# Last-token matrices turned in block 0, the last two MoE blocks summed on 128 partitions, the last expert staged, and the final scaling shared with GpSimd

## The reference

```python
yb = lax.map(expert_block, ...)       # (silu(x @ w_gate[e]) * (x @ w_up[e])) @ w_down[e]
y_slot = yb[dest] * wts.reshape(-1)[order][:, None]
ffn = jax.ops.segment_sum(y_slot, tok, num_segments=n_tok)
x = x + gate2 * ffn.reshape(bsz, L, D_MODEL)
# final: y = x * rsqrt(mean(x * x) + eps) * norm_f_w
```

## Time and profile before

| | |
|---|---|
| median of 3 runs | 1455.46 us (1450.97 to 1467.53) |
| profiled execution | 1452.0 us |
| its span, first to last instruction | 1449.7 us |
| mean granted TensorE clock | 0.969 of full |
| PE matmul busy | 1358.5 us, 94% |
| DVE, ACT, POOL busy | 433.9, 265.5, 234.1 us |
| chain that ended last | PE 79%, DMA 8%, DVE 5%, issue 3% |
| DMA in total | 318.07 MB, mean 219 GB/s |

### The profile page before, as it was taken

How to read it: one execution, slowest core, us unless ns; L and a number is a source line. 1 busy time by engine, 2 the same in 40 slices (tenths; PEclk the granted TensorE clock), 3 DMA queues, 4 the chain that set the end, 5 groups by cost and what they waited for, 6 DMA issues and landing times.

```text
span 1449.7 us, 26021 instructions
## 1 busy us (share of the span) xinstructions
PE 1358.5 (94%) x10242; PEld 850.3 (59%) x10243; DVE 433.9 (30%) x913; ACT 265.5 (18%) x401; POOL 234.1 (16%) x280
## 2 busy tenths in 40 slices
PE   5898999978999999999969999999999999999975
PEld 3688778756787666664434455555555455554532
DVE  4792860375622412104462000000000000000065
ACT  3305012244125000000111111111111111111102
POOL 0043402200000000000005013003122222222320
PEclk9899899998999999999989999999999999999997
DMA  7459622345430212413168818917949999999993
GB/s 302 152 136 386 140 69 66 81 147 181 170 111 10 87 44 73 172 46 145 44 249 330 342 29 340 395 29 292 396 155 396 389 398 380 403 380 403 377 402 132
DMA packets 91756, 318.07 MB, mean 219 GB/s; under 512 B 11920, under 2 KB 12304, under 8 KB 91440
## 3 DMA queue, kind: packets, MB, share of 16 engines
q1 hardware_dynamic: 72304, 268.77, 48.9%
q0 software_dynamic: 10608, 34.19, 8.0%
q10 hardware_dynamic: 8784, 14.24, 3.2%
HBM read 281.99 MB, written 33.06 MB: 217 GB/s over the span
## 4 chain that ended last, share of the span: by engine, by line
PE 79%; DMA 8%; DVE 5%; issue 3%; ACT 2%; SPq 2%; POOL 0%; POOLq 0%; DVEq 0%; ACTq 0%
PE ps L2222 22%; PE ps L1762 11%; PE ps L2233 11%; PE ps L1750 10%; DMA expert_w<-in_w_down 5%; PE ps L2132 5%; PE ps L2183 4%; PE ps L1854 2%; PE ps L1937 2%; DMA expert_w<-in_w_up 2%; SPq L553 1%; PE ps L2228 1%; PE ps L2212 1%; PE ps L1777 1%; DMA x_sorted<-h,router_ints 1%
## 5 line engine op out<-in xcount | busy, mean ns | idle before, releaser
L2222 PE MATMUL ps<-expert_w,x_block_t 128*64 128x256 f32 x3584 | 405.8, 383 | 10.6 <-issue 6.7
L2222 PEld LDWEIGHTS ps<-expert_w,x_block_t 128*64 128x64 f32 x3584 | 257.2, 138 | 159.1 <-issue 33.7
L2233 PE MATMUL ps<-expert_w,act_t 128*64 128x512 f32 x896 | 212.7, 602 | 4.1 <-DMA expert_w<-in_w_down 3.7
L1762 PE MATMUL ps<-h_t,weight_ring 128*128 128x320 f32 x640 | 179.0, 436 | 0.1
L1762 PEld LDWEIGHTS ps<-h_t,weight_ring 128*128 128x128 f32 x640 | 121.6, 191 | 54.2 <-issue 7.6
L1750 PE MATMUL ps<-h_t,weight_ring 128*128 128x320 f32 x512 | 148.8, 454 | 2.8 <-ACT h_t L730 2.8
L1661 DVE TENSOR_TENSOR activations<-silu_tmp,ps 128x256 f32<-128x256 f32 x56 | 23.6, 422 | 375.7 <-ACT silu_tmp L948 375.6
L1750 PEld LDWEIGHTS ps<-h_t,weight_ring 128*128 128x128 f32 x512 | 102.0, 201 | 46.7 <-issue 9.3
L2233 PEld LDWEIGHTS ps<-expert_w,act_t 128*64 128x64 f32 x896 | 58.3, 137 | 101.4 <-issue 81.4
L673 POOL COPY expert_w<-staged 128x1024 f32<-128x1024 f32 x42 | 43.8, 1043 | 416.8 <-PE ps L2222 315.9
L1682 DVE COPY y_block<-ps 128x512 f32<-128x512 f32 x25 | 17.3, 692 | 187.5 <-PE ps L2233 187.5
(11 more groups left out here) (355 smaller groups left out, 1309.1 us busy)
## 6 DMA issues: line engine op xcount, KB each, us to landing
expert_w<-in_w_down SPq DMA_DIRECT2D x128, 512.0 KB, 13.6
weight_ring<-in_stream SPq DMA_DIRECT2D x98, 512.0 KB, 5.0
expert_w<-in_w_gate SPq DMA_DIRECT2D x58, 512.0 KB, 11.3
expert_w<-in_w_up SPq DMA_DIRECT2D x58, 512.0 KB, 12.3
staged<-in_w_gate SPq DMA_DIRECT2D x28, 512.0 KB, 13.9
gathered<-in_w_gate SPq DMA_DIRECT2D x28, 512.0 KB, 15.9
gathered<-in_w_up SPq DMA_DIRECT2D x28, 512.0 KB, 16.5
x_sorted<-zero POOLq DMA_DIRECT2D x18, 512.0 KB, 15.0
```

What stands on the lines that cost most here:

```text
L1762: last = mm(pair(job)[:, a, :], w[:, k, :], h_t[:, k, a * HALF:(a + 1) * HALF], start=(k == 0), stop=(k == KD - 1))
L2222: last = mm(ps[MB * g:MB * g + MB, 2 * half + w, 0:256], x_blk_t[:, 2 * kp + k2, :], rows[:, at_col:at_col + 256], start=(kp == 0 and k2 = ...
L2233: last = mm(ps[MB * half:MB * half + MB, 4, :], act_t[:, 4 * (f // 4) + 2 * (f % 2) + f // 2 % 2, :], w_slot[3 * f + 2][:, 4 * half:4 * ha ...
```

## The change

- The last expert is loaded like all others (`next_expert(n)` for n up to 15), with POOL's copies for it too. POOL's gathers therefore wait for `slot_filled >= EXPERTS * STAGED`, the last of these copies.
- The matrices of the last tokens are turned in block 0, behind the down slice 5, into banks 0 to 2, and DVE copies them. `pick_t` moves to memory that is free from then on.
- Block 26's result is copied to `y_blk` like the others'. SP then copies its two halves with two DMAs to the other half of the partitions (`y_swap`), and DVE multiplies them by the gate into the other half of `y_last` (`take_swapped`). So block 26 and block 27 stand on different partitions for the same columns, and one matmul with 128 partitions adds both: five chunks with two matmuls each, in banks 0, 2, 6, 4, 0.
- The 20 gather steps are spread as `((0, 0, 6), (2, 4, 8))`.
- In the final norm the reciprocals of two chunks come together; chunks 0, 2 and 4 are scaled by DVE, chunks 1 and 3 by POOL in two operations.

```diff
@@ SP
-                if staged == 0:
-                    for f in range(STAGED // 2):
-                        sp.wait_ge(gu_in[f], 64)
-                        sp.sem_inc(slot_filled, 2)
...
-            with sp.Fori(2, EXPERTS - 1) as n:
-                next_expert(n, STAGED)
-            with sp.Fori(EXPERTS - 1, EXPERTS) as n:
-                next_expert(n, 0)
+            with sp.Fori(2, EXPERTS) as n:
+                next_expert(n)
+            sp.wait_ge(y_raw_ready, 1)
+            for half in range(2):
+                sp.dma_start(y_swap[MB * (1 - half):MB * (2 - half), :], y_blk[MB * half:MB * half + MB, :])\
+                    .then_inc(y_swapped, 16)
             for c in range(CH):
-                sp.wait_ge(fin_ready, c + 1)
+                sp.wait_ge((fin_ready, fin_pool)[c % 2], c // 2 + 1)
@@ POOL
-            with pool.Fori(1, EXPERTS - 1) as n:
+            with pool.Fori(1, EXPERTS) as n:
...
-            pool.wait_ge(slot_filled, (EXPERTS - 1) * STAGED)
+            pool.wait_ge(slot_filled, EXPERTS * STAGED)
...
+            for c in (1, 3):
+                pool.wait_ge(std_inverse, c + 1)
+                nc.gpsimd.tensor_scalar(fin[c][:, :], fin[c][:, :], rms2[:, 24 + c:25 + c], None, ALU.mult)\
+                    .then_inc(pool_scaled, 1)
+                pool.wait_ge(pool_scaled, c // 2 + 1)
+                nc.gpsimd.tensor_tensor(fin[c][:, :], fin[c][:, :], nf_row[:, :], ALU.mult).then_inc(fin_pool, 1)
@@ ACT
-            act.wait_ge(pick_turned, 1)
-            turned = pick_t[:, :, :, :].rearrange("p u c t -> p (u c t)")
-            nc.scalar.activation(turned[:, 0:512], ps[:, 7, :], ACT.Copy)
...
@@ DVE
-                note(vec.tensor_tensor(pick[:, u, :, 0, :], hit1, hit2, ALU.add))
-                note(vec.tensor_tensor(pick[:, u, :, 1, :], hit1, hit2, ALU.add))
+                for half in range(2):
+                    note(vec.tensor_tensor(pick[:, half, :, u if half else 1 - u, :], hit1, hit2, ALU.add))
...
+            def take_swapped():
+                for half in range(2):
+                    rows = slice(MB * (1 - half), MB * (2 - half))
+                    note(vec.tensor_tensor(y_last[rows, half, :, :], bc(y_swap[rows, :], 1, 2),
+                                           g2_row[rows, :, 512 * half:512 * half + 512], ALU.mult))
...
+            dve.wait_ge(pick_turned, 1)
+            turned = pick_t[:, :, :, :].rearrange("p u c t -> p (u c t)")
+            vec.tensor_copy(turned[:, 0:1024].rearrange("p (a n) -> p a n", a=2), ps[:, 0:2, :])
+            vec.tensor_copy(turned[:, 1024:1280], ps[:, 2, 0:256]).then_inc(pick_taken, 1)
...
-            for u, (ahead, beside, behind) in enumerate(((0, 0, 6), (3, 6, 5))):
+            for u, (ahead, beside, behind) in enumerate(((0, 0, 6), (2, 4, 8))):
                 add_some(ahead)
                 dve.wait_ge(silu_ready, last2 * 2 + (2 * u + 1))
                 take_prod(0)
+                if u == 1:
+                    dve.wait_ge(y_swapped, 32)
+                    dve.wait_ge(slot_filled, EXPERTS * STAGED)
+                    take_swapped()
                 add_some(beside)
                 dve.wait_ge(silu_ready, last2 * 2 + (2 * u + 2))
                 take_prod(1)
                 add_some(behind)
                 dve.wait_ge(down_done, last2 * KF + (u * KF + KF))
-                take_last(u, 0)
-                take_last(u, 1)
-                dve.wait_ge(y_last_ready, 2 * u + 2)
-                vec.nop().then_inc(y_copied, 1)
...
+                if u == 0:
+                    dve.wait_ge(y_stored, last2 * 32 + 32)
+                    vec.tensor_copy(y_blk[:, :], ps[:, 4, :]).then_inc(y_copied, 1)
+                    dve.wait_ge(y_copied, last2 + 2)
+                    vec.nop().then_inc(y_raw_ready, 1)
+            settle()
+            take_last(0)
+            take_last(1)
...
+            add_last_rows(0)
+            add_last_rows(1)
+            invert(0)
+            invert(1)
+            scale_rows(0)
+            add_last_rows(2)
+            add_last_rows(3)
...
@@ PE
+                if f == KF - 3:
+                    pe.wait_ge(pick_ready, 1)
+                    for n in range(2 * CH):
+                        last = nc.tensor.transpose(ps[:, n // 4, (n % 4) * P:(n % 4 + 1) * P],
+                                                   pick[:, n // CH, n % CH, :, :].rearrange("p a t -> p (a t)"), ident)
+                    last.then_inc(pick_turned, 1)
...
+            for c in range(CH):
                 cv = 0 if c < SCH else 1
-                pe.wait_ge(y_last_ready, 2 * u + cv + 1)
+                pe.wait_ge(y_last_ready, (1, 1, 1, 2, 2)[c])
+                if c == CH - 1:
+                    pe.wait_ge(x3_ready, 1)
                 for half in range(2):
...
+                    last = mm(ps[:, (0, 2, 6, 4, 0)[c] + half, :], pick_t[:, half, c, :], y_last[:, half, cv, :],
+                              start=True, stop=True)
```

79 lines of the change are left out of this document (35 added, 44 removed).

## The result

The changed kernel takes 1470.69 us (median of 18 runs, 1463.25 to 1481.38) against 1453.91 us for the kernel before on the same chip (18 runs, 1449.04 to 1467.53): a ratio of 1.0117, 95% interval 1.0094 to 1.0139. It is 1.2% slower. I had said 1458, with a chance of 0.83 that the change stays within 1% of no difference; the range ended at 1470. The profiled execution took 1467.5 us with a span of 1465.7, 16.0 more than before.

A forecast was written before the change was run, and what follows sets the result against it. DMA was taken to bound the kernel up to the last product, a serial chain after it. 0 + 9.6 - 7.9 + 2.4 = +4.1 on 1452.0 gave 1456.1, or 1459.6 on the median; forecast 1458, range 1447 to 1470.

The forecast's parts named there:

- the swapped rows: Block 26's result swapped for DVE late in block 27: landing between 1411.3 and 1417.4, taken as 1412.0.
- the first sum: Ahead of the first final add: four matmul records of 0.45 us, 1.8 us, and 0.2 to hand over.
- Gathers and evacuation: Last two blocks: late gathers hold DVE, so the last block's evacuation starts at 1431.5, not 1421.9: +9.6 us.
- From evacuation to the first add: After the last product: half the evacuation and the transposes leave the path, 11.3 us becomes 3.4: -7.9.
- Final scaling: First final add to last scaling, shared by DVE and POOL: 13.46 us becomes 15.9, +2.4 (1.6 to 4).
- The tail: After the last scaling: no term in the sum; the last store's 3.05 us was noted in the kernel before.
- block 0's transposes: Ten transposes added in block 0, 1.3 us of PE time, absorbed by later waits for weights: taken as 0.
- the loop end: PE's 3.1 us of empty block-loop iterations lie beside the wait for DVE; in the open, the saving is 6.1.
- (a): Rival: gathers land quicker, 6.5 us in place of 10.1; 1449 profiled, 1452 on the median; chance 0.17.
- (b): Rival: DVE isn't held at all and the changed end stands alone, -17.6 us, 1438 on the median; chance 0.04.
- (d): Rival: transfers unchanged, DVE's delay and the saved end cancel, 1455 to 1456; chance 0.10.
- (c): Rival: same wait but longer, evacuation after 1442, +11.1 on top; 1467 profiled, 1471 median; chance 0.14.

The follow-up runs named there:

- e4: The kernel before with the last expert staged and nothing else, so the gathers go late; ratio 1.0047 to the kernel before.
- e7: The changed kernel with the last expert loaded directly as before and the two swap DMAs on ACT's queue; ratio 1.0053 to the kernel before.
- e3: The changed kernel with the last expert loaded directly as before, so the gathers go early; ratio 1.0119 to the kernel before.
- e10: The changed kernel with the last expert loaded directly, the swap DMAs on ACT's queue and the final scaling on DVE alone; ratio 0.9980 to the kernel before.
- e1: The changed kernel with the final norm back on DVE alone; ratio 1.0068 to the kernel before.
- e8: The changed kernel with all 20 gather steps put behind the last block's second product; ratio 1.0191 to the kernel before.
- e12: The changed kernel with the gather steps last, as in e8, and the swap DMAs on ACT's queue; ratio 1.0089 to the kernel before.
- e2: The kernel before with the shared final scaling on POOL and DVE added and nothing else; ratio 1.0046 to the kernel before.
- e9: The changed kernel with POOL scaling chunk 1 only and DVE taking chunk 3; ratio 1.0081 to the kernel before.

## Why the prediction was wrong

The hold ahead of the evacuation was foreseen; what failed is the pricing of the end behind it. The sum gave POOL's share of the final norm +2.4 us, and nothing for POOL's drain at the program's end. These two steps measured +5.9 (1.1 of it by the TensorE clock) and +4.05, and make up 7.6 us of the miss. The rest lies in two other terms: the swapped rows came later than I said, and the first sum took twice its time, 2.4 and 2.0 us.

On the profiled time the sum said +4.1 and +15.5 were measured (1452.0 to 1467.5). The gap of 11.4 lies in four terms.

**Gathers and evacuation, +9.6 said, +12.0 measured.** The mechanism was right nearly to the instruction: last copy 1388.7 said and 1387.4 measured, first gather 1389.1 and 1388.2, first scaling 1399.2 and 1398.66, first half product 1410.3 and 1409.73, PE standing over 10 us ahead of its turn. The 2.4 us come from the swapped rows: I put them at 1412.0, between 1411.3 and 1417.4, and they were there at 1414.20 (6.63 us from the second issue). That pushed chunk 2's end and so chunk 4's gather, from 1419.5 to 1421.9. These times flatter the forecast a little: everything from block 26 on was 1.4 us earlier in this execution than in the one that I reckoned from, and on that count the evacuation was 13.4 us late, not 12.0. The mechanism stands on it as well. That the time is this hold and not something else that happened with it is shown by e4 (the hold alone costs 9.3 us in the profile, 0.5% in time) and by e7 (without it and the swap's place on the queue the evacuation is back at 60.5). What I missed is that the swap on SP's queue becomes a hold of the same size once the last expert is loaded directly and the gathers are early: e3.

**From evacuation to the first add, -7.9 said, -5.9 measured.** The evacuation's half took 1.54 (1.4 said). The sum took from 1435.41 to 1439.27, 3.86, where I said 2.0. I had divided 5.43 us by twelve records and given each of the four new records that pace. But the old records have 64 rows and run in pairs side by side; a new one has 128. The groups of all forty records before and all twenty now (busy us, mean ns) show half the records in the same time.
```profile
L2311 PE MATMUL ps<-y_last,last_tokens_t 64*128 64x512 f32 x40 | 11.9, 743 | 2.4 <-ACT last_tokens_t L990 1.5 <-DVE final L1707 0.9
```
```profile
L2347 PE MATMUL ps<-y_last,last_tokens_t 128*128 128x512 f32 x20 | 11.8, 755 | 6.6 <-DVE y_last L1658 6.6
```
The comparison holds only at one clock, and both sums began at the lower level. In these windows the clock stands behind the five busy times, first the kernel before, then the changed one:
```profile
1427.00:1433.00 6.00, 5.26 (x14) 2.22 (x16) 0.00 (x0) 2.18 (x4) 0.00 (x0) 0.51 0.00 0
```
```profile
1435.00:1440.00 5.00, 4.59 (x6) 2.02 (x7) 2.37 (x4) 0.00 (x0) 0.00 (x0) 0.50 0.00 0
```
At that level a pair of 64-row records starts every 0.85 us before, and a single 128-row record every 0.85 now; where the clock is back at 1.00, both do every 0.43. So four new records need 3.9 us to the first add at the lower level, and at the upper one they would need about the 2.0 that I said, by luck, as my pace was that of the pairs at the lower. In the changed kernel the PE had stood 6.65 us ahead of the sum. In e10, where it had stood 3.31, the sum began at 1.00, fell to 0.50 after 1437, and the first add came 2.54 us after its start. The join on 128 partitions saves PE no time; in exchange it needs the swap.

**Final scaling, +2.4 said (1.6 to 4), +5.9 measured.** The range was wrong too. I took the multiply by the per-row scalar at one copy's time, 1.04, without a word on it, and bounded only the second operation, at 3.1. The second took 2.35, near my 2.1; the first took 3.80. POOL is done with chunk 3 at 18.3 after the first add, where I had 14.6, and DVE's last scaling, which starts at 16.0, takes 3.33 beside it. "GPSIMD Engine Reference" of the Trainium skill, Elementwise, by which I had estimated 2.25 for the two-input multiply, is near the measured 2.35. For the 3.80 I had no row.

The 3.80 isn't shown to be the operation's time alone. In all thirteen instances, in seven kernels, one of DVE's scalings was under way when it began, and ended 1.07 to 1.10 us later; the scalings that had begun ahead of POOL took no longer than alone (1.27 against 1.28 in e1). If POOL stood still for that time, as DVE does behind POOL's multiply by `norm_f`, the operation would take 2.7 alone; that is an estimate, and no run has it without a scaling of DVE. I had priced the turns on DVE's side only.

Not all of the +5.9 is POOL's. 1.1 us of it come from the sum of chunk 1, which at the lower clock was 2.78 us behind that of chunk 0, where I had 1.8. In e3, e8 and e12, with the same join and the same work on POOL but this sum only 1.64 to 1.83 us behind, the stretch takes 18.2 to 18.4; in e2, without the join, 17.9. e2 shows most of the term, 4.5 us, without the rest of the change.

**The tail, 0 said, +4.05 measured.** It wasn't in my sum. I gave the last store its 3.05 us and didn't ask what else the end of the program waits for. POOL, which used to go into its drain 46 us before the end, now works until 1457.5, a microsecond before DVE is done with the last chunk. e1, e2 and e9 show it from three sides.

Together 2.4 + 2.0 + 3.5 + 4.05 = 11.95, less 0.5 that lies outside the span (1.8 us now, 2.3 before).

**Right:** block 0's transposes cost nothing that can be seen. Block 2's gates start 58.2 us after the first scatter before and 57.7 after. From the scatter to block 26 it is 603.2 and 603.3, but this figure scatters by 3.3 us between the kernels, more than the 1.3 of the transposes; the DMA rate didn't change; the loop end is hidden by the late evacuation.

**The rivals.** (a) and (b) didn't happen: the first landing was 10.4 us after the first issue. (d) was true of the transfers but not of the rest. (c) named 1467 on the profiled time, and 1467.5 came, but not by its mechanism: it wanted the evacuation after 1442 (its own terms, added up, reach only 1441.0), and it came at 1433.9. The other terms, for which I had allowed 1.6 us in it, made the difference. Its chance, 0.14, was too low because I put all doubt into the waits and hardly any into the operations that no row showed.

**Open.** From the first add on POOL's share costs 9.9 us in the profile by e1, 8.5 by e2 and 8.7 by e10 against e7, the first with the 1.1 us of the clock in it. The timed ratios give 7 us for e1 and e2 and 10 for e10 against e7, and their intervals, some 5 us on either side with two ratios and 3.5 with one, don't tell these apart. What POOL's multiply by the per-row scalar takes alone isn't shown. Nor is it shown why the clock in the first sum differs between executions of one kernel.

## What to carry to other kernels

When a buffer is lent to a second user, ask what its first user is now late for, and then what is late next: here the late gathers held the end by some 10 us, and going back to direct loads alone gave nothing, as the swap then waited behind the weights for as long. An engine that is given work near the end brings its operations, the slowdown of the engines beside it, and its own wind-down at the program's last line; price all three. A small transfer on which the chain hangs belongs on a queue without bulk loads. And an operation that the trace doesn't show needs bounds that are really wide, one for each operation.

## What I had not expected of the hardware

- POOL's multiply of 128x1024 float32 by one value per partition took 3.80 us, each time with one of DVE's scalings under way for its first 1.1 us; its multiply of two such tiles took 2.35, its copy 1.04.
- POOL's drain at the program's end took 10.3 us and ended 7.9 to 8.0 us after its last operation in three kernels (changed, e2, e9).
- Two 128 KB transfers, from the first issue to their use, took 7.2 us behind weights whose last issue was 14 us before them (changed), 15.0 and 18.9 us right behind 4 MB of weights on the same queue (e3, e8), and about 8 us on another queue in the same traffic (e7, e12).
- Two float32 matmuls of 64 rows each ran side by side at the pace of one of 128, a start every 0.85 us at the lower clock level and every 0.43 at the upper: forty records in 11.9 us, twenty in 11.8.
- The Trainium skill ("SBUF — State Buffer", Who interferes with whom) says that a DVE operation with two SBUF inputs and a GpSimd operation that reads SBUF take turns. These rows agree: 1.28 us alone (e1), 2.11 and 3.33 where DVE's scaling began beside POOL's two-input multiply, each ending 1.07 to 1.08 us after it.
